# Side loads of a recurrent scan: four large transfers cut into twenty pieces, each issued behind a phase of a step

## The reference

```python
def step(S, inp):
    r_t, w_t, k_t, v_t, kk_t, b_t = inp
    sa = jnp.einsum('bhvk,bhk->bhv', S, kk_t)
    S = S * w_t[:, :, None, :] - sa[..., None] * b_t[:, :, None, :] + v_t[..., None] * k_t[:, :, None, :]
    return S, jnp.einsum('bhvk,bhk->bhv', S, r_t)
...
y = (y + bonus.reshape(B, T, D_RWKV)) * g                     # after a group norm of y
out = jnp.einsum('btc,cd->btd', jnp.concatenate([attn_out, rwkv_out], axis=-1), lp['w_out'])
x = x + g1[:, None, :] * mix
```

## Time and profile before

| what | value |
|---|---|
| median of 3 runs | 1185.63 us (1185.29 to 1186.04) |
| the profiled execution | 1185.35 us |
| its span in the trace | 1183.5 us |
| mean granted PE clock | 0.914 |
| PE busy | 989.1 us (84%) |
| DVE busy | 432.3 us (37%) |
| scan block, steps 1 to 9 | 474.7 to 644.3 us of the span |

### The profile page before, as it was taken

The page is one execution under the profiler, slowest core; times in us unless marked ns, Lnnn a source line. Parts: engine busy times, 40 slices in busy tenths (PEclk is TensorE's granted clock), DMA queues, the critical chain, the costliest instruction groups (busy, mean ns, idle before and its releaser), DMA issues. The chain is left out here.

```text
span 1183.5 us, 18268 instructions
## 1 busy us (share of the span) xinstructions
PE 989.1 (84%) x7714; PEld 591.1 (50%) x7714; DVE 432.3 (37%) x853; ACT 275.2 (23%) x518; POOL 84.8 (7%) x133
## 2 busy tenths in 40 slices
PE   3699999978777745978798998299999999999970
PEld 0265555535455545877786555244444444444430
DVE  1402642132488845573854655400010010000006
ACT  2311222224566521222112112001111111111101
POOL 0320000010000020212120000200000000000003
PEclk9899999989699977988797999599999999999995
DMA  9713352639999020205021721696899898998907
GB/s 342 240 24 141 103 182 73 214 118 403 408 404 401 13 47 2 57 20 135 12 65 41 299 71 71 252 352 248 308 351 334 322 351 320 334 350 313 332 35 266
DMA packets 97188, 247.16 MB, mean 209 GB/s; under 512 B 7252, under 2 KB 12148, under 8 KB 96608
## 3 DMA queue, kind: packets, MB, share of 16 engines
q1 hardware_dynamic: 85664, 218.64, 50.5%
q0 software_dynamic: 5632, 13.97, 4.3%
q10 hardware_dynamic: 5824, 13.55, 2.9%
HBM read 176.51 MB, written 67.01 MB: 206 GB/s over the span
## 5 line engine op out<-in xcount | busy, mean ns | idle before, releaser
L2125 PE MATMUL ps<-arena 128*128 128x512 f32 x544 | 239.2, 597 | 1.7 <-ACT arena L2175 1.7
L2125 PEld LDWEIGHTS ps<-arena 128*128 128x128 f32 x544 | 102.5, 191 | 126.6 <-issue 125.8
L2139 PE MATMUL ps<-arena 128*128 128x512 f32 x272 | 121.3, 598 | 3.6 <-ACT arena L2179 3.6
L696 PE MATMUL ps<-arena 128*128 128x512 f32 (+3 forms) x448 | 123.6, 435 | 0.0
L696 PEld LDWEIGHTS ps<-arena 128*128 128x128 f32 (+1 forms) x448 | 67.7, 188 | 60.2 <-issue 59.3
L2139 PEld LDWEIGHTS ps<-arena 128*128 128x128 f32 x272 | 50.7, 192 | 62.1 <-issue 62.1
L1794 PE MATMUL ps<-arena 128*128 128x512 f32 x160 | 72.3, 605 | 1.9 <-PEq L1253 1.9
L2216 DVE TENSOR_TENSOR arena<-arena,ps 128x512 f32<-128x512 f32 x17 | 11.7, 688 | 136.8 <-ACT arena L2171 136.8
L563 DVE SCALAR_TENSOR_TENSOR arena<-arena 128x128 f32<-128x128 f32 (+3 forms) x56 | 30.9, 552 | 82.6 <-ACT arena L440 81.1
L2224 DVE COPY arena<-ps 128x512 f32<-128x512 f32 x17 | 11.8, 692 | 125.9 <-PE ps L2139 125.9
L630 PE MATMUL ps<-arena 128*128 128x512 f32 (+1 forms) x160 | 52.4, 485 | 0.0
(11 more groups left out here) (311 smaller groups left out, 1362.0 us busy)
## 6 DMA issues: line engine op xcount, KB each, us to landing
gathered_tokens<-arena SPq DMA_DIRECT2D x16, 2560.0 KB, 26.2
arena<-in_exp_up_dram SPq DMA_DIRECT2D x17, 2048.0 KB, 18.1
arena<-in_exp_gate_dram SPq DMA_DIRECT2D x17, 2048.0 KB, 13.1
arena<-in_exp_down_dram SPq DMA_DIRECT2D x17, 2048.0 KB, 9.9
arena<-in_w_mod_dram SPq DMA_DIRECT2D x12, 2048.0 KB, 13.6
arena<-gathered_tokens SPq DMA_DIRECT2D x18, 512.0 KB, 15.1
expert_outputs<-arena ACTq DMA_DIRECT2D x17, 512.0 KB, 8.1
arena<-in_w_in_dram SPq DMA_DIRECT2D x4, 2048.0 KB, 7.9
```

The lines of the kernel that those rows point to most:

```text
L696: mm = pe.matmul(ps[0:m, b, 0:hi - lo], ring[:, slot_of(what), k, (e % 4) * P:(e % 4) * P + m], hT[:, k, lo:hi], start=(k == 0), stop=(k = ...
L2125: mm = pe.matmul(ps[:, b, :], xgT[:, k, :], w[u][:, k, :], start=(k == 0), stop=(k == KT - 1))
L2139: mm = pe.matmul(ps[:, Y0 + half, :], hidT[:, k, :], wd[u][:, k, half * 512:(half + 1) * 512], start=(k == 0), stop=(k == 3))
```

## The change

The four loads become twenty pieces: `gate1` in 4 halves of a row of 1024 (256 KB each), `wout` in 8 row blocks of 256 KB (the first four as two transfers of 64 partitions), `bonus2` and `attnX` in 4 blocks of 640 columns (320 KB each). SP now walks through the steps and waits, ahead of each piece, for one phase of that step: `rhs_mm` (steps 4 and 5 only), `d1_mm`, `l5_mm` and `d2_mm`. Gates go in steps 2 and 3, output weights in 4 and 5, the bonus in 6 and 7, the attention in 8 and 9; where a step has one piece it goes behind `d1_mm`. The state store moves from step 2 to step 3. The engines that use the data wait for the higher counts. The bytes are the same, the number of these transfers goes from 7 to 24.

```diff
+        def wout_piece(sp, n):
+            if n < NC4:
+                for g in range(2):
+                    at = 256 * g + 64 * n
+                    sp.dma_start(wout[64 * g:64 * g + 64, 0, n], w_out[0][at:at + 64, 0:512]).then_inc(ld_wout[0], 16)
+            else:
+                at = D_ATTN + P * (n - NC4)
+                sp.dma_start(wout[:, 0, n], w_out[0][at:at + P, 0:512]).then_inc(ld_wout[0], 16)
...
-                sp.wait_ge(y_mm, steps_until(0, 0, 4))
-                load_wout(sp, 0)
-                sp.wait_ge(y_mm, steps_until(1, 7, NCH))
-                sp.dma_start(bonus2.rearrange("p a t -> p (a t)"), bonus_d).then_inc(ld_bo, 16)
-                sp.wait_ge(y_mm, steps_until(1, 4, 7))
-                sp.dma_start(attnX.rearrange("p a t -> p (a t)"), attn_d).then_inc(ld_at, 16)
+                for s in range(2, STEPS):
+                    sp.wait_ge(y_mm, s)
+                    if s in (4, 5):
+                        sp.wait_ge(rhs_mm, s + 1)
+                        wout_piece(sp, 4 * (s - 4))
+                    for k, done in enumerate((d1_mm, l5_mm, d2_mm)):
+                        if s in (3, 7, 9) and k:
+                            continue
+                        sp.wait_ge(done, s + 1)
+                        if s in (2, 3):
+                            n = k if s == 2 else 3
+                            half = slice(512 * (n % 2), 512 * (n % 2) + 512)
+                            sp.dma_start(gate1[:, n // 2, half], mod_d[n // 2, half].partition_broadcast(P)).then_inc(ld_g1, 16)
+                        elif s in (4, 5):
+                            wout_piece(sp, 4 * (s - 4) + 1 + k)
+                        else:
+                            a4 = k if s in (6, 8) else 3
+                            to, src, got = (bonus2, bonus_d, ld_bo) if s < 8 else (attnX, attn_d, ld_at)
+                            sp.dma_start(to[:, a4], src[:, a4 * T:(a4 + 1) * T]).then_inc(got, 16)
...
-                act.wait_ge(ld_bo, 16)
+                act.wait_ge(ld_bo, 64)
...
-                pe.wait_ge(ld_at, 16)
-                pe.wait_ge(ld_wout[0], 48)
+                pe.wait_ge(ld_at, 64)
+                pe.wait_ge(ld_wout[0], 192)
...
-                        dve.wait_ge(ld_g1, 32)
+                        dve.wait_ge(ld_g1, 64)
```

More of the change, by code:

```diff
@@ L1258, in _ @@
                         sp.dma_start(rows(stage_in[:, z], p), state_rwkv[0, 0, z].rearrange("(j p) v k -> p v j k", p=2)[p]).then_inc(ld_state, 16)
[L1259 to L1265, removed]
@@ L1266, in _ @@
-                sp.wait_ge(y_mm, steps_until(0, 0, 4))
-                load_wout(sp, 0)
-                sp.wait_ge(y_mm, steps_until(1, 7, NCH))
-                sp.dma_start(bonus2.rearrange("p a t -> p (a t)"), bonus_d).then_inc(ld_bo, 16)
-                sp.wait_ge(y_mm, steps_until(1, 4, 7))
-                sp.dma_start(attnX.rearrange("p a t -> p (a t)"), attn_d).then_inc(ld_at, 16)
+                assert steps_until(1, 0, 2) <= 2 and steps_until(0, 0, 4) <= 4
+                assert steps_until(1, 7, NCH) <= 6 and steps_until(1, 4, 7) <= 8
@@ new lines, in _ @@
+                for s in range(2, STEPS):
[17 more added lines that the diff above has]
+                            sp.dma_start(to[:, a4], src[:, a4 * T:(a4 + 1) * T]).then_inc(got, 16)
+                    if s == 3:
+                        sp.wait_ge(so_ok, 1)
+                        for z in range(2):
+                            for p in range(2):
+                                sp.dma_start(new_state[0, 0, z].rearrange("(j p) v k -> p v j k", p=2)[p], rows(stage_out[:, z], p)).then_inc(st_state, 16)
```

## The result

| | before | after |
|---|---|---|
| median | 1186.04 us (5 runs, 1185.29 to 1190.93) | 1177.81 us (5 runs, 1174.56 to 1177.92) |
| profiled execution | 1185.35 us | 1177.92 us |
| its span | 1183.5 us | 1176.1 us |

The ratio of the two is put at 0.9923, with a 95% interval of 0.9903 to 0.9942 (the medians alone give 0.9931): the change makes the kernel faster by 0.6 to 1.0%. The forecast was 1177.2 us.

A forecast was written before the change was run, and what follows sets the result against it. PE bounds the kernel (989.1 of 1183.5 us), stalled in the scan by instruction refills behind bulk loads. Gains 5.0 + 0.7 + 2.9 - 0.2 = 8.4 us take 1185.35 to 1176.95; 0.28 added gives 1177.2, range 1173.5 to 1182.5.

The forecast's parts named there:

- The mechanism: In the scan, refills of PE's instructions stand behind bulk loads, stalling PE up to 5.43 us and lowering its clock.
- the refills are not held by the loads: Rival, chance 0.09: the long idle times in the scan come from PE's own stream and stay; no change, 1185.6 us.
- The landings that the prediction leaned on: Scan loads of output weights, bonus and attention: PE resumed 0.2 to 0.3 us behind each landing, three times.
- Step 4: Scan step with `diag_blocks` where output weights loaded whole: 5.0 us less, with 1.0 us taken off for pieces.
- The 1.0 us I took off: Loss assumed in scan step 4 because a piece runs as the `diag_blocks` begin and may delay a refill.
- Steps 5 and 6: Scan steps with a substitution on DVE, bonus loaded in the first: together 0.7 us less, bounds 0 and 1.0.
- The bound of 1.0: Most that scan steps 5 and 6 could gain, from what DVE can save: 25.65 - 24.64 = 1.01 us.
- Step 8: Scan step where the attention loaded whole: becomes like step 7, 2.9 us less, bounds 0 and 3.13.
- Clean steps: Scan steps 3, 7 and 9, which receive pieces or the state store: 0.2 us lost in all, bounds 0 and 3.1.
- The sum: All terms over the scan: 5.0 + 0.7 + 2.9 - 0.2 = 8.4 us less.
- More transfers: SP issues 17 transfers more in the scan, at 0.3 to 0.6 us each, with nothing else to do: cost 0.

## Why the prediction was right

- **The mechanism.** Refills of PE's instructions were held back by the bulk loads. The load in step 7 and the copy within HBM show it: the stall goes where the bulk goes, and needs no write into the core's memory; and every such stall ends 1.2 to 1.9 us behind the end of a refill. The rival "the refills are not held by the loads" is out. The landings that the prediction leaned on were not the link. The refill stood behind the load's packets, as it had it, but only behind one transfer or two: with four in place of one it came 1.3 to 1.6 us earlier, past some 0.5 MB that was still queued. The rule of the Trainium skill ("DMA: Bandwidth & Descriptors", Queues, rings and completion order) is out as I had applied it, that a refill waits for one of the packets that the profile counts: 128 of them, the whole load, began ahead of it in step 8. The same section puts a packet at some 9 to 17 descriptors, and whether the profile counts such packets is not shown, so the runs refute my use of the rule and not the rule.
- **Step 4** was forecast at 5.0 us less and gave 5.72. The 1.0 us I took off for a piece in a refill's way was not there: stall 1.15, as without any load (1.31 in two kernels). The size of the gain is less firm: in the change's second trace step 4 took 19.87 us at a stall of 1.19, which is 4.09 less than before.
- **Steps 5 and 6** were forecast at 0.7 and gave 0.94. DVE had the end, as read: over the stretch that was read in the earlier trace rows, which ends where DVE starts on the right sides of step 6, it took 24.65 us (557.57 to 582.22) and not 25.65, the 1.0 that it was said to be able to save. PE's stall of 1.97 us in `cross` went, and 1.91 us of waiting for DVE ahead of `inner` took its place, so the 1.97 would have been wrong as the gain. The bound of 1.0 was no bound, though: other kernels had steps 4 to 6 at the same 58.2 to 58.8 us with the pair at 38.7 to 38.9, when the dip of the clock fell into step 4 and not into step 6.
- **Step 8** was forecast at 2.9 and gave 3.13. **Clean steps** were charged 0.2 and lost nothing in steps 7 and 9 (14.32 and 14.80 us, before 14.32 and 14.88).
- **The sum** of these was larger than forecast, 9.8 against 8.4, and the time still came out 0.6 us above the forecast. Most of the difference stands ahead of every load, and 0.24 us in steps 1 to 3: step 1 began at 476.72 and not 474.67, and step 0, which no piece touches, took 18.86 us at a clock of 0.75 against 16.70 at 0.90. The change's second trace began step 1 at 474.35, so this is not of the change. It was a term of noise of some 2 us that the prediction did not name. That the total came so near is partly luck: parts that were 1.4 us better met noise of 2 us the other way.
- **More transfers** cost nothing, as forecast. The batching rule of the Trainium skill ("DMA: Bandwidth & Descriptors", Bandwidth: batch transfers to 1 MiB or more) agrees with the landings, four pieces of 3.0 us each against 8.4 for the whole, and decides nothing here, because no engine waits for them.

## What to carry to other kernels

An idle time of PE that nothing in the profile releases, with the DMA engines full, may be PE waiting for its own program: look for the instruction queue's packets in that stretch, and compare the step with a twin that has no load in it. First rule out a wait in the code that the profile does not name: here PE's idle times ahead of `inner` were marked the same way and were DVE's, as 0.1 us between DVE's end and PE's start shows. Cut a large background load into transfers of some 300 KB or less, or place it where PE has to wait anyway; both gave the same here, and waits between the pieces added nothing that could be timed. A stall of one microsecond can cost two or three when the clock falls behind it (stall 1.01, step longer by 2.47).

## What the runs showed of the hardware

- One transfer of 1280 KB, into the core's memory or between two places of HBM, delays the first refill of PE's instructions in step 7 or 8 to 4.5 to 5.3 us into the step, where it comes 1.1 to 1.8 us into it with no load running; two transfers of 640 KB do so to 4.7 us, and four of 320 KB back to back, with SP's queue alone at 92 to 96% of the engines' time, to 3.2 to 3.6 us.
- PE goes on 1.2 to 1.6 us behind the end of the refill's packet (53 stalls; once 1.87). Without any load, too, the run of small `diag_blocks` stalled: 1.0 to 1.7 us in step 1 over the thirteen traces, 1.31 in step 4 in the two kernels that had no load there.
- The size of the packets, 2560 or 10240 bytes, moved the stall by 0.7 us within one transfer and by some 0.3 at most within four, which is no more than two traces of the same load differ by.
- The same steps of the same kernel vary with where the clock dips: step 4 of the changed kernel took 18.24 us at 0.91 and 19.87 at 0.83 in two traces, with stalls of 1.15 and 1.19, and step 1 began anywhere from 473.1 to 480.2 us over thirteen traces of kernels that differ only behind it (one also in the layout of a scratch tensor). A difference in time under 0.2% needs the steps to be compared, not the totals.
